# First layer begun with the values' projections, late modulation in buffers of its own, gated groups in four PSUM banks

## The chip, the cores and the metric

One core of one Trainium2 chip. The metric is the device time of one execution in microseconds (us). The engines are TensorE (PE), VectorE (DVE), ScalarE (ACT), GpSimd (POOL) and SyncE (SP), which issues every DMA of this kernel. Each runs its own instruction stream in order; semaphores tie them together. Everything is float32.

## The reference

A first block of two layers ("ab" and "cd") over 512 tokens x and 256 context tokens ctx, width 1024, and then a second block of two layers of feed-forward, mixing, feed-forward. The change touches only the first block; cut to that:

```python
def _adaln(cond, w_mod, b_mod):
    return jnp.split(jax.nn.silu(cond) @ w_mod + b_mod, 3, axis=-1)      # shift, scale, gate
def _post_norm(x, y, gate, g, b):
    return _layer_norm(ALPHA * x + gate * y, g, b)
def _ab_mixer(h, w_in, pool_w, pool_scale, sgu_w, sgu_b, w_out):
    a, ga, u, v, gb = split(h @ w_in)                                     # five times 512 columns
    ya = _multiscale_pool(a, pool_w, pool_scale) * jax.nn.silu(ga)        # windows 2, 4, 8, 16
    yb = _chunk_sgu(u, v, sgu_w, sgu_b) * jax.nn.silu(gb)                 # v normalized by head
    return jnp.concatenate([ya, yb], axis=-1) @ w_out
def first_block(x, c, ctx, c_ctx, ...):
    # layer ab
    sh, sc, gt = _adaln(c, ab_w_mod, ab_b_mod);  csh, csc, cgt = _adaln(c_ctx, ab_w_mod, ab_b_mod)
    y  = _ab_mixer(x * (1 + sc) + sh, ...);      yc = _ab_mixer(ctx * (1 + csc) + csh, ...)
    ctx = _post_norm(ctx, yc, cgt, ab_ln_g, ab_ln_b);  x = _post_norm(x, y, gt, ab_ln_g, ab_ln_b)
    # layer cd: Fourier mixing and latent attention, x attends to ctx and x
    h = x * (1 + sc2) + sh2;  hc = ctx * (1 + csc2) + csh2
    y = _cd_out(f_in, f_gate, attn, d_gate, cd_fnet_w, cd_w_out)
    return _post_norm(x, y, gt2, cd_ln_g, cd_ln_b)
```

## The kernel before

**Products.** Every dense product is taken in two parts: an operand is split into hi (ACT copies it to float32r) and lo (DVE subtracts hi from the operand), and PE does three matmuls, hi x hi, hi x lo, lo x hi (`mm3`). A weight chunk is 1024 x 256 (1 MB): SP loads it into one of two `raw` buffers, ACT makes `w_hi`, DVE makes `w_lo` (`split_at`, lines 1367 and 1785), into one of two pairs. `raws_to(n)` on SP loads up to chunk n, and waits before each load until the chunk two before it is split. ACT waits for the last use of the pair. Activations are held by feature, as `h_hi`, `h_lo` (x) and `ctx_hi`, `ctx_lo`.

**Order.** There is no scheduler in the first block: each engine's program is written out by hand, and a `Signal` counts events. PE takes PSUM banks from a ring of eight (`rot`); `claim` waits until the last holder of a bank was freed. ACT and DVE share three `work` tiles, given out by the list `work_order`.

**Layer ab.** (1) Eight modulation products of 1 MB of weights each (`mod_product`; weights into six `mod_w` buffers, then the last two), each turned to features (`mod_turn`); they give shift and scale. (2) Four x tiles of 128 tokens are turned by PE and scaled and split by ACT and DVE (`turn`). (3) Ten chunks of `ab_w_in` in order 0 to 9: chunks 0, 1 are the pool's input (kept in `pooled_in`), 2, 3 its gate, 4, 5 u, 6, 7 the values v, 8, 9 the second gate. A chunk other than 6 and 7 is four groups: two halves of 128 features, each for x (512 columns, 24 matmuls) and ctx (256 columns, 24 matmuls). Chunks 6, 7 are six token tiles each, with the weights as the moving operand; DVE then takes statistics and norm for each of 24 (chunk, tile, head) in turn, with POOL's power for the deviation. The ctx tiles are turned within chunk 0. (4) Sixteen late modulation products (`late_product`, numbers 8 to 23, the gate of ab and all of cd) lie between the groups; their weights go to `late_w`, which borrows the room of `u_gated` and `v_norm`, and for four of them to `raw`. (5) Meanwhile POOL makes the window means of `pooled_in`. (6) The middle: eight `pool` groups (g, r), where r = 0 is x and r = 1 ctx, and eight `sgu` groups; for each DVE multiplies by the gate, ACT makes hi, DVE makes lo, and only then comes the next. (7) Four chunks of `ab_w_out`, out-chunks 0 to 3: x tile i fills banks 2i and 2i+1; chunks 0 and 1 for all four tiles, then 2 and 3 tile by tile. The finished tile is called y(i). Then the same for ctx, with the layer norms (`AB_TAIL`) on DVE and ACT and turns of the normalized tiles back to features.

**Layer cd.** Eight chunks of `cd_w_in`. The ctx tiles are turned (`c_turn`) inside chunk 0; chunk 1 has two gate rows (PE multiplies a matrix of ones by diagonals that DVE builds at line 1837, `gate_diags`). POOL applies the gain and bias rows of ab's norm to X (lines 2404 and 2406). At the end of cd each tile's norm runs DVE statistics, POOL power, ACT normalize (line 1420), DVE gain (1874), POOL bias (2427), ACT square (1427), POOL power, DVE scale (1881), PE turn (815), while PE works on the next tile.

## Time and profile before

| | |
|---|---|
| median of 3 runs | 2972.14 us (2970.36 to 2980.99) |
| the profiled execution | 2969.76 us |
| its span, first to last instruction | 2968.0 us |
| PE, DVE, ACT, POOL busy | 94%, 39%, 32%, 6% |
| mean granted TensorE clock | 0.961 |

A matmul's end is modelled and matmuls are pipelined, so busy PE is not PE at its peak. The clock is given as a share of 2.4 GHz; the other level is 1.2 GHz. PEld is the weight load beside the matmul; SPq is the time of SP's DMA issue. "idle before <- X" names what ended an engine's idle time. L745 is the line of every matmul, so groups are told apart by tiles.

### The profile page before, as it was taken

The page shows a single profiled execution, that of the slowest core. Times are in us where ns is not written, and L with a number is a line of the kernel's source. Part 1 is how long each engine was busy: PE and PEld are TensorE (multiplying, and loading weights), DVE is VectorE, ACT ScalarE, POOL GpSimd, SP SyncE. Part 2 cuts the span into 40 slices and gives each one's busy share as a digit, 9 for nine tenths or more (in the row PEclk, how much of TensorE's full clock was granted, in tenths as well). Part 3 has the DMA queues.
Part 4 walks back from the last instruction along what each step waited for, and adds up shares of the span by engine and source line. Part 5 has one row for each costly group of instructions (what it writes and reads, how often), then busy time and mean ns, then how long its engine had stood idle before and what let it go on. Part 6 is the DMA issues. An engine that isn't in the chain of part 4 may idle for free.

```text
span 2968.0 us, 34969 instructions
## 1 busy us (share of the span) xinstructions
PE 2775.1 (94%) x14803; PEld 2220.0 (75%) x14803; DVE 1167.1 (39%) x1745; ACT 962.9 (32%) x1433; POOL 180.0 (6%) x291
## 2 busy tenths in 40 slices
PE   4998779998799999998799999999999998899998
PEld 2877668565688888776488888888888775688887
DVE  2123563255433324444643332433324445633322
ACT  2211232343232223545432222322225355332221
POOL 0130030000100000000000000000001000100000
PEclk7998989999899999998799999999999998899999
DMA  7432222002033323211123323223232111123321
GB/s 248 143 110 71 86 88 74 29 1 65 29 114 99 100 95 96 70 44 57 43 72 100 99 97 117 86 89 97 99 114 76 57 43 43 54 96 100 100 100 71
DMA packets 208000, 250.06 MB, mean 84 GB/s; under 512 B 6351, under 2 KB 187174, under 8 KB 207846
## 3 DMA queue, kind: packets, MB, share of 16 engines
q1 hardware_dynamic: 207846, 247.83, 25.9%
q8 instruction: 118, 1.93, 0.3%
q14 instruction: 36, 0.29, 0.0%
...
## 4 chain that ended last, share of the span: by engine, by line
PE 84%; DVE 6%; ACT 4%; issue 3%; POOL 1%; SPq 1%; DMA 1%; DVEq 0%; POOLq 0%; ACTq 0%
PE psum L745 81%; PE psum L1207 1%; PE psum L815 1%; PE psum L1128 1%; POOL stats_first L2362 1%; DVE w_lo L1785 1%; ACT w_hi L1367 1%; DMA mod_w<-in_ab_w_mod 0%; DVE h_lo L1794 0%; SPq L637 0%; DVE spare_lo L1785 0%; DVE v_norm L1958 0%; POOL X L2427 0%; ACT softplus L1737 0%; DVE stats_first L1861 0%
## 5 line engine op out<-in xcount | busy, mean ns | idle before, releaser
L745 PE MATMUL psum<-h_hi,w_hi 128*128 128x512 f32 (+1 forms) x2096 | 791.1, 377 | 28.1 <-issue 15.0
L745 PE MATMUL psum<-h_lo,w_hi 128*128 128x512 f32 (+1 forms) x2096 | 781.8, 373 | 0.0
L745 PE MATMUL psum<-h_hi,w_lo 128*128 128x512 f32 (+1 forms) x2096 | 781.3, 373 | 0.0
L1785 DVE TENSOR_TENSOR w_lo<-raw,w_hi 128x2048 fp32r<-128x2048 f32 (+1 forms) x176 | 400.0, 2275 | 767.2 <-ACT w_hi L1367 766.9
L745 PEld LDWEIGHTS psum<-h_hi,w_hi 128*128 128x128 f32 x2096 | 400.3, 191 | 106.4 <-issue 28.6
L745 PEld LDWEIGHTS psum<-h_hi,w_lo 128*128 128x128 f32 x2096 | 399.7, 191 | 68.5
L745 PEld LDWEIGHTS psum<-h_lo,w_hi 128*128 128x128 f32 x2096 | 400.3, 191 | 67.2 <-issue 1.2
L1367 ACT ACTIVATE w_hi<-raw 128x2048 fp32r<-128x2048 f32 (+1 forms) x176 | 332.6, 1892 | 219.1 <-PE psum L745 214.3
L1376 ACT ACTIVATE work<-psum 128x512 f32<-128x512 f32 (+3 forms) x184 | 91.5, 503 | 412.0 <-PE psum L745 348.0
L745 PE MATMUL psum<-w_hi,ff_hi 128*128 128x512 f32 x576 | 224.6, 390 | 0.0
L745 PE MATMUL psum<-w_lo,ff_hi 128*128 128x512 f32 x576 | 224.1, 389 | 0.0
L745 PE MATMUL psum<-w_hi,ff_lo 128*128 128x512 f32 x576 | 224.1, 389 | 0.0
L745 PE MATMUL psum<-w_hi,h_hi 128*128 128x256 f32 (+2 forms) x512 | 168.6, 329 | 27.5 <-DVE w_lo L1785 13.1
L1655 ACT ACTIVATE ff_hi<-work 128x512 fp32r<-128x512 f32 (+1 forms) x96 | 57.3, 597 | 367.8 <-DVE work L2183 367.8
L745 PE MATMUL psum<-w_lo,h_hi 128*128 128x256 f32 (+2 forms) x512 | 162.6, 318 | 0.0
L745 PE MATMUL psum<-w_hi,h_lo 128*128 128x256 f32 (+2 forms) x512 | 162.1, 317 | 0.0
L745 PEld LDWEIGHTS psum<-w_hi,h_hi 128*128 128x128 f32 x512 | 101.3, 198 | 41.8 <-issue 15.2
L2183 DVE TENSOR_TENSOR work<-work,psum 128x512 f32<-128x512 f32 (+1 forms) x96 | 61.7, 643 | 165.3 <-PE psum L745 165.2
L745 PEld LDWEIGHTS psum<-w_hi,ff_lo 128*128 128x128 f32 x576 | 108.1, 188 | 22.6
L745 PEld LDWEIGHTS psum<-w_hi,ff_hi 128*128 128x128 f32 x576 | 108.1, 188 | 22.4
L745 PEld LDWEIGHTS psum<-w_lo,ff_hi 128*128 128x128 f32 x576 | 108.1, 188 | 22.0
L745 PEld LDWEIGHTS psum<-w_hi,h_lo 128*128 128x128 f32 x512 | 100.9, 197 | 5.9
...
## 6 DMA issues: line engine op xcount, KB each, us to landing
raw<-in_ffn_w_gate SPq DMA_DIRECT2D x44, 1024.0 KB, 5.3
raw<-in_ffn_w_up SPq DMA_DIRECT2D x44, 1024.0 KB, 5.3
raw<-in_ffn_w_down SPq DMA_DIRECT2D x44, 1024.0 KB, 4.8
...
raw<-in_ab_w_in SPq DMA_DIRECT2D x10, 1024.0 KB, 5.2
mod_w<-in_ab_w_mod SPq DMA_DIRECT2D x8, 1024.0 KB, 11.7
raw<-in_w_out SPq DMA_DIRECT2D x8, 1024.0 KB, 4.9
raw<-in_cd_w_in SPq DMA_DIRECT2D x7, 1024.0 KB, 5.4
```

What stands on the lines that cost most here:

```text
L745: return pe.matmul(o, lhsT, rhs, start=start, stop=stop, skip_group_check=True)
L815: m = pe.transpose(bank(b, P, j * P), wide[1][:, k * P:(k + 1) * P], ident[:, :])
L1128: m = pe.transpose(bank(b + k // 4, P, (k % 4) * P), probs[(n - 1) % 2][:, k * P:(k + 1) * P], ident[:, :])
L1207: m = pe.transpose(bank(b, P, k * P), src[:, k * P:(k + 1) * P], ident[:, :])
L1367: act.activation(split_tiles(key)[0][:, 0:nk * n], raw[c % 2][:, 0:nk * n], ACT.Copy).then_inc(*w_hi_made.mark(key))
L1376: act.activation(o, src, func, **kw).then_inc(*kept.mark(name or event))
L1655: act.activation(ff_hi[:, k, off:off + n], work[used.index((k, half_)) % 3][:, 0:n], ACT.Copy).then_inc(*ff_hi_made.mark(event))
L1785: dve.tensor_tensor(lo[:, 0:nk * n], raw[c % 2][:, 0:nk * n], hi[:, 0:nk * n].bitcast(F32), ALU.subtract).then_inc(*w_lo_made.mark(key))
L2183: dve.tensor_tensor(w, w, full(event, n), ALU.mult).then_inc(*gated.mark(event))
L2362: pool.tensor_tensor(o, a, half[:, 0:n], ALU.pow).then_inc(*rsqrt_made.mark(event))
```

## The change

- **Order of chunks.** 6, 7, 0, 1, 2, 3, 4, 5, 8, 9. The order on PE, ACT and DVE comes from one list, `AB_STEPS`. Values are projected tile by tile for both chunks as soon as an x tile is turned; turns of the tiles and late modulations 8 to 13 lie between. Numbers 14 to 21 lie in chunks 0 and 1, 22 and 23 in chunk 2.
- **DMA.** The wait of SP for the vectors' turn goes. All eight modulation weights have buffers and are issued first; X comes in four tiles with a weight chunk between; late modulation weights have three buffers (`u_gated`, `silu_ga`, one of its own) and leave `raw`.
- **Values' norm.** Four heads of a tile at once: four statistics, four aggregates, one bias, one power on POOL, four norms.
- **Weight splits.** Each is placed one chunk ahead (`split`), also those of chunks 8 and 9.
- **Middle.** Groups in banks 4 to 7, r = 0 before r = 1; product n+1 comes before lo n on DVE. PE does the output tiles 0 and 1 of out-chunks 0 and 1 between them. Out-chunk 2's spare tiles are free after the pool groups.
- **cd.** Context turns after chunks 0 and 1, not inside; gate diagonals behind a weight split; the gain and bias rows of X on DVE in chunks 1 and 2. At the end of cd the norm is two DVE instructions, (x - mean) g and then times the deviation plus b; ACT's and POOL's parts go.

```diff
+AB_STEPS = [("turn", 0), ("turn", 1), ("v", 6, 0), ("v", 7, 0), ("turn", 2), ("mod", 8), ("v", 6, 1), ("v", 7, 1), ("turn", 3), ("mod", 9),
+            ("v", 6, 2), ("v", 7, 2), ("turn", 4), ("mod", 10), ("v", 6, 3), ("v", 7, 3), ("turn", 5), ("mod", 11), ("sgu_w",),
+            ("v", 6, 4), ("v", 6, 5), ("end", 6), ("split", 0), ("mod", 12), ("v", 7, 4), ("v", 7, 5), ("end", 7), ("mod", 13)]
+for _i, _ch in enumerate((0, 1, 2, 3, 4, 5, 8, 9)):
+    if _ch < 9:
+        AB_STEPS.append(("split", (1, 2, 3, 4, 5, 8, 9)[_i]))
+    for _j in range(2):
+        for _r in range(2):
+            AB_STEPS.append(("group", _ch, _j, _r))
+            if _ch < 2:
+                AB_STEPS.append(("mod", 14 + 4 * _ch + 2 * _j + _r))
+            if _ch == 2 and _r == 0:
+                AB_STEPS.append(("mod", 22 + _j))
+            if _ch in (4, 5) and _r == 0:
+                AB_STEPS.append(("gate", _ch - 4, _j))
+    AB_STEPS.append(("end", _ch))
+AB_MID = [(kind, g, r) for kind in ("pool", "sgu") for r in range(2) for g in range(4)]
...
-            sp.wait_ge(*psum_full["vecs"])
-            for n in range(6):
+            for n in range(8):
                 sp.dma_start(mod_w[n][:, :, :], mod_chunk("ab_w_mod", n * CW)).then_inc(*mod_landed[n].mark(n))
+            for t in range(NT):
+                sp.dma_start(X[:, t, :], A["x"][0, t * P:(t + 1) * P, :]).then_inc(*x_landed[t].mark("all"))
+                if t == 1:
+                    raws_to(0)
+            raws_to(1)
             sp.dma_start(CTX[:, :, :], A["ctx"][0].rearrange("(t p) d -> p t d", p=P)).then_inc(*ctx_landed.mark("all"))
...
             def late(m):
-                s = m % 2 if m < 8 else 1
-                if m > 1:
-                    sp.wait_ge(*psum_full["modp", 8 + (m - 2 if m < 8 else m - 1)])
+                s = m % 3 if m < 14 else 0
+                before = {14: 12, 15: 14}.get(m, m - 3)
+                sp.wait_ge(*psum_full["modp", 8 + before if m > 2 else 7])
...
+            for m in range(3):
+                late(m)
+            sp.dma_start(sgu_w[:, :, :], A["ab_sgu_w"][0].rearrange("h i j -> i h j")).then_inc(*sgu_w_landed.mark("all"))
...
+            raws_to(3)
+            for m in range(3, 8):
+                late(m)
+            raws_to(4)
+            late(8)
+            late(9)
+            raws_to(5)
+            for m in range(10, 14):
+                late(m)
+            raws_to(6)
+            inv_count(0)
+            raws_to(7)
+            late(14)
+            late(15)
+            inv_count(1)
+            raws_to(8)
+            inv_count(2)
+            inv_count(3)
+            raws_to(9)
             raws_to(CHUNK["ab_out", 0] + 2)
             sp.wait_ge(*h_lo_made["sgu", 3, 1])
...
-            raws_to(CHUNK["cd_in", 0] + 3)
-            sp.wait_ge(*h_lo_made["ct", NC - 1, 1])
+            raws_to(CHUNK["cd_in", 0] + 5)
+            sp.wait_ge(*ln_made["ab_x", NT - 1])
...
+            for r in range(2):
+                for g in range(4):
+                    pool_group(g, r)
             for c in range(2):
                 begin(("ab_out", c))
-                for i in range(NT):
+                for i in range(2):
+                    m = out_part("ab_x", c, i, i * P)
+                if c == 0:
+                    pe.wait_ge(*sgu_w_turned["all"])
+                    pe.wait_ge(*v_normed[5])
+                for hd in range(4):
+                    sgu_group(hd, c)
+            for c in range(2):
+                for i in range(2, NT):
                     m = out_part("ab_x", c, i, i * P)
                 done(m, ("chunk", "ab_x", c))
...
-                act.wait_ge(*h_lo_made["sgu", 3, 1])
+                act.wait_ge(*h_lo_made["pool", 3, 1])
...
+            def v_norms(t):
+                heads = [4 * t + hd for hd in range(4)]
+                places = [full(("v", 6 + hd // 2, t), P, hd % 2 * P) for hd in range(4)]
...
+                for i, ps in zip(heads, places):
+                    m = dve.bn_stats(stat("v", i, 0, 6), ps)
...
+                bias_variance(("v", t), v_stat(t, 7), 1.0)
+                dve.wait_ge(*rsqrt_made["v", t])
+                for hd, i, ps in zip(range(4), heads, places):
+                    m = dve.tensor_scalar(v_norm[:, t, hd * P:(hd + 1) * P], ps, stat("v", i, 6, 7), stat("v", i, 8, 9), ALU.subtract, ALU.mult)
...
+            for n, event in enumerate(AB_MID):
+                if event == ("sgu", 0, 0):
+                    split_at(CHUNK["ab_out", 1])
...
+                mid_product(event)
+                if n:
+                    mid_lo(AB_MID[n - 1])
...
             for ch in range(8):
+                if ch:
+                    split_at(CHUNK["cd_in", ch] + 1)
                 if ch == 1:
                     for j in range(2):
                         gate_diags(("gate_cd", j), mod_cd, j, 0)
-                if ch:
-                    split_at(CHUNK["cd_in", ch] + 1)
+                if ch in (1, 2):
+                    x_rows(2 * ch - 2)
+                    x_rows(2 * ch - 1)
+                if ch < NC:
+                    turn("ct", ch, h_hi, h_lo, L + ch * P, scale_odd[:, :, 1], shift_odd[:, :, 1])
...
+                if s == "cd":
...
+                    dve.scalar_tensor_tensor(out=tile, in0=tile, scalar=stat("ln", i, 12, 13), in1=g_row[:, :], op0=ALU.subtract,
+                                             op1=ALU.mult).then_inc(*residual.mark(("gain", s, t)))
+                    dve.wait_ge(*residual["gain", s, t])
+                    dve.wait_ge(*rsqrt_made["ln", s, t])
+                    dve.scalar_tensor_tensor(out=tile, in0=tile, scalar=stat("ln", i, 14, 15), in1=cd_b[:, :], op0=ALU.mult,
+                                             op1=ALU.add).then_inc(*ln_put.mark(t))
+                    return
```

## Rows read from the trace of the kernel before

**Rows 1.** Busy time by stage: PE, PEld, DVE, ACT, POOL, then clock, DMA share, GB/s.
```profile
0.00:67.90 67.90, 24.01 (x194) 14.01 (x194) 16.44 (x39) 18.84 (x37) 3.19 (x7) 0.80 0.75 245
67.90:294.80 226.90, 212.13 (x1384) 177.40 (x1384) 58.62 (x156) 43.40 (x70) 48.73 (x50) 0.95 0.35 114
294.80:355.00 60.20, 43.49 (x206) 33.55 (x206) 31.65 (x50) 16.46 (x22) 0.00 (x0) 0.89 0.31 105
401.30:445.70 44.40, 31.13 (x118) 23.71 (x118) 30.24 (x37) 13.97 (x22) 21.55 (x10) 0.81 0.40 127
```

**Rows 2.** Timeline of the start (start us, us, engine, line, op; idle before).
```profile
6.17 11.31 SPq L637 DMA_DIRECT2D mod_w<-in_ab_w_mod  x6
11.56 2.77 PE L745 MATMUL psum<-mod_w,silu_c 128*32 128x256 f32 x16 [5.42 <-DMA mod_w<-in_ab_w_mod]
44.99 2.77 PE L745 MATMUL psum<-mod_w,silu_c 128*32 128x256 f32 x16 [16.40 <-DMA mod_w<-in_ab_w_mod]
67.90 0.77 PE L745 MATMUL psum<-h_hi,w_hi 128*128 128x512 f32 x1 [13.31 <-issue]
```

**Rows 3.** Timeline of PE, end of chunk 5.
```profile
187.53 0.80 PE L745 MATMUL psum<-h_hi,w_hi 128*128 128x512 f32 x1
193.47 1.49 PE L745 MATMUL psum<-v_norm,silu_c 128*32 128x256 f32 x16
194.89 0.38 PE L745 MATMUL psum<-ctx_hi,w_hi 128*128 128x256 f32 x1
197.86 0.50 PE L745 MATMUL psum<-mod_sum,mod_row 96*128 96x2 f32 x4
```

**Rows 4.** Timeline of DVE, first head of the values.
```profile
201.38 0.30 DVE L1951 BATCH_NORM_STATS2 stats_first<-psum 128x6 f32<-128x128 f32 x1 [2.04 <-PE psum L745]
202.76 0.41 DVE L1958 TENSOR_SCALAR v_norm<-psum,stats_first 128x128 f32<-128x128 f32 x1 [0.67 <-POOL stats_first L2362]
```

**Rows 5.** Waits of PE, 190 to 300 (us in total, times, longest).
```profile
PE psum L745 <- DVE w_lo L1785: 14.8, 3, 6.0
```

**Rows 6.** Timeline of DVE, the gated groups.
```profile
299.50 0.74 DVE L1991 SCALAR_TENSOR_TENSOR work<-psum,cols,silu_ga 128x512 f32<-128x512 f32 x1
318.68 0.69 DVE L1794 TENSOR_TENSOR h_lo<-work,h_hi 128x512 fp32r<-128x512 f32 x1 [0.69 <-ACT h_hi L1411]
333.90 0.42 DVE L1794 TENSOR_TENSOR ctx_lo<-work,ctx_hi 128x256 fp32r<-128x256 f32 x1 [0.48 <-ACT ctx_hi L1411]
```

**Rows 7.** Timeline of the middle: PE's first output tile, the fourth out-chunk's hi.
```profile
324.23 0.77 PE L745 MATMUL psum<-w_hi,h_hi 128*128 128x512 f32 x1 [11.37 <-issue]
343.92 1.92 ACT L1367 ACTIVATE spare_hi<-raw 128x2048 fp32r<-128x2048 f32 x1 [7.57 <-DMA raw<-in_ab_w_out]
```

**Rows 8.** Timeline of DVE: gate diagonals of either layer, a context split.
```profile
155.23 0.88 DVE L1837 TENSOR_SCALAR work<-ident,mod 128x128 f32<-128x128 f32 x4
421.20 4.27 DVE L1794 TENSOR_TENSOR ctx_lo<-work,ctx_hi 128x512 fp32r<-128x512 f32 x2 [2.64 <-ACT ctx_hi L1403]
430.92 5.81 DVE L1837 TENSOR_SCALAR work<-ident,mod_odd 128x128 f32<-128x128 f32 x8
```

**Rows 9.** Waits of PE, 345 to 470.
```profile
PE psum L745 <- DVE work L1837: 10.0, 1, 10.0
PE psum L799 <- DVE work L1854: 3.1, 1, 3.1
```

**Rows 10.** Timeline of the first tile's norm at the end of cd.
```profile
744.71 1.23 DVE L1874 TENSOR_TENSOR X<-X,g_row 128x1024 f32<-128x1024 f32 x1 [1.31 <-ACT X L1420]
746.08 2.42 POOL L2427 TENSOR_TENSOR X<-X,b_row 128x1024 f32<-128x1024 f32 x1 [2.87 <-DVE X L1874]
752.14 1.94 PE L815 MATMUL psum<-ident,wide 128*128 128x128 f32 x8 [3.29 <-DVE wide L1881]
```

**Rows 11.** The page's costliest groups: the low half of a weight split.
```profile
L1785 DVE TENSOR_TENSOR w_lo<-raw,w_hi 128x2048 fp32r<-128x2048 f32 (+1 forms) x176 | 400.0, 2275 | 767.2 <-ACT w_hi L1367 766.9
```

**Rows 12.** DMA issues, 0 to 500 (KB each, median us to landing).
```profile
raw<-in_ab_w_in SPq DMA_DIRECT2D x10, 1024.0 KB, 5.2
```

More of the change, by code:

```diff
@@ L115, in add @@
         plan.append(what)
-    for ch in range(10):
+    for ch in (6, 7, 0, 1, 2, 3, 4, 5, 8, 9):
         add(("ab_in", ch), "ab_w_in", 0, "cols", ch * CW, CW, True)
-        if ch > 5:
-            w, c0 = LATE_MOD[6 + ch]
-            add(("mod", 14 + ch), w, 0, "cols", c0, CW, False)
     for c in range(4):
@@ L870, in tensor_program @@
             mod_turn(7)
-            pe.wait_ge(*x_landed["all"])
-            for t in range(NT):
-                turn("xt", t, X[:, t, :])
             open_turn = []
@@ L925, in tensor_program @@
-                end(("ab_in", ch))
-            pe.wait_ge(*raw_landed[CHUNK["mod", 23] % 2][CHUNK["mod", 23]])
-            late_product(23, raw[CHUNK["mod", 23] % 2][:, :].rearrange("p (k n) -> p k n", n=CW))
-            close_turn()
-            pe.wait_ge(*pool_w_landed["all"])
-            pe.wait_ge(*pooled[3])
-            for g in range(4):
-                for r, (off, n) in enumerate(RANGES):
-                    b = claim(rot.take(), ("pool", g, r))
-                    done(mm(bank(b, n), pool_w[:, g, :], pooled_in[:, g, PAD_OFF[r]:PAD_OFF[r] + n], True, True), ("pool", g, r))
@@ L937, in tensor_program @@
-            pe.wait_ge(*sgu_w_turned["all"])
-            pe.wait_ge(*v_normed[7, 5, 1])
-            for hd in range(4):
-                for r, (off, n) in enumerate(RANGES):
-                    b = claim(rot.take(), ("sgu", hd, r))
-                    for q in range(n // P):
-                        m = mm(bank(b, P, q * P), v_norm[:, off // P + q, hd * P:(hd + 1) * P], sgu_wT[:, hd, :], True, True)
-                    done(m, ("sgu", hd, r))
-            def ab_ready(i, k, h):
-                if i == 0 and h == 0:
-                    pe.wait_ge(*h_lo_made[("pool", k, 1) if k < 4 else ("sgu", k - 4, 1)])
+                elif kind == "group":
+                    _, ch, j, r = step
+                    w = begin(("ab_in", ch)) if j == r == 0 else weights(("ab_in", ch))
+                    project(("ab", ch, j, r), w, j * P, P, h_hi, h_lo, *RANGES[r], rot)
+                    if (ch, j, r) == (2, 1, 1):
+                        close_turn()
+                elif kind == "gate":
+                    gate_row(("gate", step[1], step[2]))
+                elif kind == "end":
+                    end(("ab_in", step[1]))
@@ new lines, in tensor_program, with pool_group, sgu_group @@
+            mid = Ring([4, 5, 6, 7])
+            def pool_group(g, r):
+                off, n = RANGES[r]
+                b = claim(mid.take(), ("pool", g, r))
+                done(mm(bank(b, n), pool_w[:, g, :], pooled_in[:, g, PAD_OFF[r]:PAD_OFF[r] + n], True, True), ("pool", g, r))
+            def sgu_group(hd, r):
+                off, n = RANGES[r]
+                b = claim(mid.take(), ("sgu", hd, r))
+                for q in range(n // P):
+                    m = mm(bank(b, P, q * P), v_norm[:, off // P + q, hd * P:(hd + 1) * P], sgu_wT[:, hd, :], True, True)
+                done(m, ("sgu", hd, r))
@@ L950, in out_part, with ab_ready @@
+            def ab_ready(k):
+                pe.wait_ge(*h_lo_made[("pool", k, 0) if k < 4 else ("sgu", k - 4, 0)])
             def out_part(s, c, i, off):
@@ L2368, in gpsimd_program @@
             pool.memset(pooled_in[:, :, :], 0.0).then_inc(*zeroed.mark("all"))
+            for t in range(6):
+                rsqrt(("v", t), v_stat(t, 8), v_stat(t, 7), 4)
             for g, window in enumerate(POOL_WINDOWS):
```

401 lines of the change are left out of this document (172 added, 229 removed).

## The prediction

> **What bounds the kernel now.** I read the page first: TensorE (PE) is busy 94% of 2968.0 us, so only its idle and slow-clock time can be won. The diff touches the first layer and the end of the second ("cd"), so next came busy time by stage [rows 1]. PE is idle 43.9 us before its first projection at 67.9, 14.8 us inside the ten input chunks, 16.7 us between the last chunk and the first finished output tile y0 (294.8 to 355.0), and 13.3 us in the first two cd chunks. Then the timeline and the waits, to see who ends each gap.
>
> *Start* [rows 2]. The modulation products wait for data: number 6 waits 16.40 us because X, CTX and two weight chunks (5 MB) sit ahead of it. From the first landing (11.56) to that one (44.99) 11 MB come in: 3.04 us per MB, a full queue. After the last product PE stands 13.3 us while ACT and DVE scale and split four x tiles and then two weight chunks.
> *Chunks* [rows 3 to 5]. Chunks 6 and 7 (the values) make PE outrun DVE's norm chain; it waits 14.8 us in three pieces for weight splits queued on DVE behind that chain.
> *Middle* [rows 6, 7]. The gated groups are a product, ACT's hi and DVE's lo in strict turn, 34.8 us on DVE (299.50 to 334.3). PE's output tiles wait for their banks (11.37 us).
> *Start of cd* [rows 8, 9]. PE waits 10.0 us for the gate diagonals. Eight of them take DVE 5.81 us here, four took 0.88 us at 155.23; POOL is busy 21.55 us in this stage with X's gain and bias rows.
> *End of cd* [rows 10]. Each tile's chain ACT norm, DVE gain, POOL bias, ACT square, POOL rsqrt, DVE scale is longer than PE's 11 us of matmuls.
>
> **The change, part by part** (microseconds from the span's start; new kernel's times are worked out).
>
> *1. Start.* SP no longer waits for the vector rows, so modulation weights are issued some 1.9 us earlier (6.17 back to about 4.3) and all eight MB come first. First landing 9.65, the eighth 9.65 + 7 x 3.0 = 30.7. Then 2.8 us of product and turn and 1.5 us of one-plus-scale: 35. At 3.04 us per MB [rows 2] X tile 0, tile 1, weight chunk 6 land at 32.2, 33.7, 36.7, then tiles 2 and 3 and chunk 7 at 42.7, CTX at 45.8, late modulations behind. Tile 0 is scaled and split by 38.5 (an estimate: a scaling of 1.5, hi 0.6, two lo's of 0.69 [rows 6]). Chunk 6's hi (1.9) and lo (2.2) [rows 11] follow: values of tile 0 start at about **42**. Chunk 7's hi waits for its landing, its lo is done at 46.9, about when PE, cold, ends the first group. Dense work thus starts 25.9 us earlier than 67.9.
>
> *2. Values phase.* Per token tile PE has two value groups of 256 columns (24 matmuls, 2.97 each [rows 3]), one turn of x (0.95), one late modulation (1.42 + 0.37): 8.5 us. DVE has per tile four heads of statistics and norm. In turn they cost 1.7 each [rows 4], 6.8 together; batched, 4 x 0.3 + 4 x 0.2 + 0.2 + 0.7 for POOL + 4 x 0.35 make about 4.3. The x turn adds 3.2: 7.5 in all, under 8.5, with some 3 us between a tile's split and its use. So I cost the normalization at nothing. Its cover gone (1.7 a head) it costs 6 x 1.5 = 9 us. Six tiles, sgu turn and the last modulation: PE reaches chunk 0 at **94**. The banks hold: eight claims pass before a value bank is reused, by then its norm is done.
>
> *3. Chunks 0 to 5, 8, 9.* A chunk is 2 x (5.65 + 2.97) = 17.2 us [rows 3]; modulations 14 to 21 add 8 x 1.8, so chunks 0 and 1 end at 142.8. The 14.8 us of waits and about 6 us of slow clock behind them (0.95 over 226.9 us) go, since each weight split now starts a chunk ahead on a DVE with nothing behind. A new wait appears: SP queues modulation 22 behind weight chunk 5, whose buffer is free only when chunk 3 is split. That split waits for chunk 1's end (142.8), then hi 1.9 and lo 2.2: SP issues at t0+4.9. One MB lands 5.2 after issue [rows 12], the one behind it 3.04 later: t0+13.2. PE wants it at t0+5.6, so 7.6 us of stall, and the clock falls: 1.5 more. I take **9.1**; bounds 0 (if PE came later) and 12. Queued behind SP's wait there are only the next window's inverse counts, needed 100 us later. Modulation 23 is issued after product 22 and lands 3 us before PE asks. (By the Trainium skill, DMA: Bandwidth & Descriptors, the section on the anatomy of a DMA by the GpSimd path, a transfer costs about 2.0 us plus bytes at 436 GB/s; two MB would then be in at 6.8 us, the stall 6.1 instead of 7.6 and the sum 1.5 better. It is a fit for another issuing path and I go by the rows.)
> Chunk 2 then ends at 172.7, 3 at 189.9, 4 and 5 (two gate rows each, 0.8 a piece) at 227.5, 9 at **261.9**. Before it was 294.8: **-32.9**. Check by differences: -25.9 start, -14.8 waits, -6 clock, +1.8 for modulation 23 inside, +1.9 for two x turns inside, +9.1: -33.9.
>
> *4. Middle.* T is the last chunk's end. The first product on DVE still comes at T+4.8, behind a weight split (299.50 against 294.8). Pipelined, with product n+1 covering ACT's hi of n, a 512-wide pool group costs 0.74 + 0.69 instead of 2.1, a 256-wide one about 0.95. DVE: pool r=0 done T+10.2, r=1 T+14, split of out-chunk 1 T+18.2, sgu r=0 T+26.4, r=1 T+32 (27 us against 34.8). PE: tiles 0 and 1 with out-chunk 0 from T+9.8, sgu groups, out-chunk 1, tiles 2 and 3, so 22 us of output matmuls are done by T+38.8 rather than waiting for the whole chain. Out-chunk 3 is late next: SP loads it only after the last sgu lo (T+32) and behind two row loads; before, its hi started 9.6 us after that lo (334.3 to 343.92 [rows 7]). Hi 1.9 and lo 2.2 make T+46, y0 ends T+**48.8** after 4 us of stall. Before: 60.2. **-11.4**; bounds -15 (load at 5.2) and -5.
> From y0 to cd chunk 0, before 355.0 to 401.3, the order and the pieces of work are the same on every engine: 0.
>
> *5. First cd chunks.* Gain and bias rows go from POOL to DVE (8 x 1.3 = 10.3 us), in chunks 1 and 2 behind the diagonals, beside 11 us of PE per chunk whose next weights have 4 us of slack: nothing. Context turns come after whole chunks. From cd start U: DVE's last context norm U+13.8, ct turn, ACT's hi of chunk 2's weights U+20.6, lo U+23, diagonals U+23.9 (0.9 as at 155.23). PE is at the gate row at U+17.6, waits 6.3 instead of 10.0, and a wait of 3.1 in the context turns goes [rows 9]. Chunk 1 with its turn ends U+33.9 against U+44.3: **-10.4**. This rests on DVE's slow rows being POOL's doing; if they are not, 0. (The Trainium skill, SBUF — State Buffer, section "SBUF: two separate sides", says that GpSimd and a DVE instruction with two SBUF inputs exclude each other for a whole instruction. By that rule the two ctx splits, 4.27 us at 421.20 when 1.3 is usual, shrink as I assume; it also lets no such block in elsewhere, as DVE's splits beside the window sums have a chunk of slack.)
>
> *6. End of cd.* Between statistics and scaled tile, ACT's 1.24 with its two hops and POOL's 2.42 go, DVE's gain runs beside POOL's rsqrt, a second 1.29 on DVE is added: the statistics are there at 742.6 (2.1 before the gain row: 1.3 for ACT, 0.8 for POOL's rsqrt and the bias), the scaled tile at 748.8 instead of 752.0, 3.2 per tile. Four tiles make 12.8, less what PE's 11 us per tile takes back: PE's wait of 3.29 at tile 0 is all gone, the later ones shrink. **-12**, bounds -9 and -13.
>
> Sum: 32.9 + 11.4 + 10.4 + 12 = 66.7. The profiled execution took 2969.76 (1.76 around its span, 2.4 below the median 2972.14): 2969.8 - 66.7 = **2903**.
>
> **Rivals.**
> *A. Values phase bound by DVE or landings.* The chain is not shortened by batching, or data come late and the phase starts at 47. Against: the queue's pace in rows 2. 9 + 5 + some clock: 2915 to 2932.
> *B. No stall at modulation 22*, and out-chunk 3 early: 9 + 4: 2890.
> *C. Start of cd unchanged* and the middle still waits as before (the change does not do what it says there): +10.4 + 11.4: 2925; with A, up to 2940.
> *D. Slower than before.* One mechanism: late modulations starve PE. Thirteen of them (11 to 23) now hang on three buffers reloaded only after a product, in one SP queue. Slack is about 14 us after an issue. To lose 66.7 + 15 they must land 14 + 82/13 = 20 us after issue; singly they took 5.2, 11.7 only in the opening burst. At 22 us: 13 x 8 = 104, so 3007.
>
> **How the numbers follow.** Forecast (2890 to 2914) 0.57; A 0.17; C 0.09; B or better 0.10; no more than 0.5% from before 0.04; D 0.03. Half a per cent (15 us) is about what a measurement of this kernel can tell. Faster 0.93, same 0.04, slower 0.03. Leaving out the top 0.1 and the bottom 0.07, the range is 2882 to 2931.
>
> **What would show it.** First value matmul near 42; no PE wait over 1 us between 50 and 142; one wait near 148 of 5 to 9 us ended by a late modulation's DMA; last chunk's end near 262; y0 near 311 after a wait for out-chunk 3's lo; cd's gate diagonals 0.9 us for four; cd tiles 3 us apart less. Wrong if the first value matmul is after 50, or if PE waits on v_norm or h_lo in every tile.

## The result

The changed kernel takes 2907.28 us (median of 4 runs, 2906.6 to 2908.55) against 2971.25 for the kernel before on the same chip (4 runs, 2970.0 to 2980.99): ratio 0.9784, 95% interval 0.9773 to 0.9796. That is 64 us or 2.2% faster. The forecast was 2903.0 with a range of 2882 to 2931.

### The profile after, by stage

Busy time by stage of the changed kernel (columns as in [rows 1]). The stages have moved: the values' phase is 45 to 98, chunks 0 and 1 98 to 148, the other six chunks 148 to 268 (two rows), the middle 268 to 315, and most of the start of cd (359.6 to 393.8) lies in 358 to 392.

```profile
0.00:45.00 45.00, 24.41 (x178) 14.64 (x178) 7.95 (x20) 10.88 (x19) 3.18 (x7) 0.87 0.95 319
45.00:98.00 53.00, 52.36 (x436) 46.69 (x436) 32.60 (x103) 17.20 (x37) 5.07 (x5) 0.95 0.68 222
98.00:148.00 50.00, 50.00 (x357) 38.13 (x353) 8.48 (x24) 10.67 (x18) 1.85 (x2) 1.00 0.54 177
148.00:175.00 27.00, 20.23 (x97) 16.25 (x96) 2.88 (x3) 3.66 (x5) 11.38 (x10) 0.75 0.38 131
175.00:268.31 93.31, 93.21 (x539) 79.75 (x537) 18.09 (x29) 20.51 (x30) 20.16 (x17) 1.00 0.16 54
268.31:315.02 46.71, 40.98 (x186) 31.71 (x187) 30.47 (x49) 16.11 (x21) 0.00 (x0) 0.96 0.30 102
358.00:392.00 34.00, 27.81 (x114) 21.85 (x113) 21.68 (x38) 10.69 (x14) 1.10 (x2) 0.90 0.23 72
```

Against [rows 1] PE's idle time ahead of the first projection is 20.6 us and not 43.9, the queue is busy 95% of the start and not 75%, and the projections run without a gap except in one stage: between 148 and 175 PE stands 6.8 us and its clock is at 0.75. PE's own list of waits, up to 345, says who ends them (us in total, times, longest; the waits for the modulation weights and the identity matrix at the start, 10.2 and 5.7 us, are left out, and all others are 2.5 us or less):

```profile
PE psum L781 <- DMA u_gated<-in_cd_w_mod: 6.8, 1, 6.8
PE psum L781 <- DVE w_lo L1809: 4.6, 1, 4.6
PE psum L781 <- DVE spare_lo L1809: 3.1, 1, 3.1
```

The 14.8 us of waits for weight splits inside the chunks [rows 5] are gone; the one w_lo wait left is the first values' matmul. Here it is on the timeline, with what ACT and DVE did before it (start us, us, engine, line, op; idle before):

```profile
40.62 1.89 ACT L1403 ACTIVATE w_hi<-raw 128x2048 fp32r<-128x2048 f32 x1
42.55 2.29 DVE L1809 TENSOR_TENSOR w_lo<-raw,w_hi 128x2048 fp32r<-128x2048 f32 x1 [1.11 <-ACT w_hi L1403]
44.90 0.58 PE L781 MATMUL psum<-w_hi,h_hi 128*128 128x256 f32 x1 [4.64 <-DVE w_lo L1809]
```

It answers to the 67.90 of [rows 2]: 23.0 us sooner. The values' norms, one token tile with its four heads and the next tile's turn, on DVE (it answers to [rows 4]):

```profile
61.80 0.89 DVE L1963 BATCH_NORM_STATS2 stats_first<-psum 128x6 f32<-128x128 f32 x4 [1.56 <-PE psum L781]
...
64.45 1.36 DVE L1973 TENSOR_SCALAR v_norm<-psum,stats_first 128x128 f32<-128x128 f32 x4 [1.13 <-POOL stats_first L2413]
65.73 1.36 DVE L1849 TENSOR_SCALAR work<-psum,one_plus_scale,mod 128x128 f32<-128x128 f32 x4
...
70.49 0.89 DVE L1963 BATCH_NORM_STATS2 stats_first<-psum 128x6 f32<-128x128 f32 x4 [1.94 <-PE psum L781]
```

Four heads take 4.0 us from 61.80 to 65.8, a tile 8.7 us from one set of statistics to the next, and the idle time ahead of each set of statistics ends on PE: DVE waits for PE, not the other way round.

The new wait of chunk 2, on SP's and PE's timelines:

```profile
153.19 0.37 SPq L649 DMA_DIRECT2D raw<-in_ab_w_in  x1
153.60 0.58 SPq L675 DMA_DIRECT2D u_gated<-in_cd_w_mod  x1
160.88 2.35 PE L781 MATMUL psum<-u_gated,silu_c 128*32 128x256 f32 x14 [6.78 <-DMA u_gated<-in_cd_w_mod]
```

The two issues stand 0.4 us apart with weight chunk 5 in front, as the prediction read the queue. The middle's end, which answers to [rows 7]:

```profile
309.56 2.29 DVE L1809 TENSOR_TENSOR spare_lo<-raw,spare_hi 128x2048 fp32r<-128x2048 f32 x1 [6.53 <-ACT spare_hi L1403]
311.90 0.50 PE L781 MATMUL psum<-spare_hi,h_hi 128*128 128x512 f32 x1 [3.09 <-DVE spare_lo L1809]
```

The start of cd, which answers to [rows 8] and [rows 9]:

```profile
377.71 1.29 DVE L1818 TENSOR_TENSOR ctx_lo<-work,ctx_hi 128x512 fp32r<-128x512 f32 x2 [3.11 <-ACT ctx_hi L1439]
379.96 2.29 DVE L1809 TENSOR_TENSOR w_lo<-raw,w_hi 128x2048 fp32r<-128x2048 f32 x1 [0.96 <-ACT w_hi L1403]
382.17 1.65 DVE L1861 TENSOR_SCALAR work<-ident,mod_odd 128x128 f32<-128x128 f32 x8
383.18 2.04 PE L781 MATMUL psum<-work,ones 128*128 128x512 f32 x2 [6.19 <-DVE work L1861]
```

Eight diagonals take 1.65 us (5.81 before), two context splits 1.29 (4.27 before), and the gate wait is 6.2 (10.0 before). The end of cd, which answers to [rows 10]:

```profile
690.68 1.28 DVE L1895 SCALAR_TENSOR_TENSOR X<-X,stats_first,g_row 128x1024 f32<-128x1024 f32 x1
692.49 1.28 DVE L1899 SCALAR_TENSOR_TENSOR X<-X,stats_first,b_row 128x1024 f32<-128x1024 f32 x1 [0.52 <-POOL stats_first L2413]
697.40 1.06 PE L851 MATMUL psum<-ident,wide 128*128 128x128 f32 x8 [0.39 <-DVE wide L1911]
```

PE's wait there was 3.29 and is 0.39; over the four tiles its waits for the scaled tile are 16.2 us before and 7.3 after.

### Where the time came from

To compare stages I follow six marks on DVE's timeline through both kernels: the last gated product of chunk 9; the statistics of the first output tile's norm (y0); of the second context norm; of cd's first and last norm; and the last residual addition of the first feed-forward. Each time is the start of that instruction.

| mark | before | after | gained in this stage |
|---|---|---|---|
| last gated product of chunk 9 | 295.4 | 268.8 | 26.6 |
| y0's norm | 358.0 | 317.8 | 13.6 |
| second context norm | 412.6 | 370.8 | 1.6 |
| cd's first norm | 740.9 | 689.0 | 10.1 |
| cd's last norm | 793.8 | 732.6 | 9.3 |
| first feed-forward's last addition | 1165.6 | 1101.0 | 3.4 |
| mixing of layer 0, addition to addition | 358.5 long | 353.8 long | 4.7 |
| mixing of layer 1 | 351.1 long | 358.1 long | -7.0 |

64.6 us are won by 1101; 62.4 arrive in the span (2968.0 against 2905.6). The difference is in the two mixing stages, whose code did not change; more on that below. The 1.6 us between y0 and the context norm are no gain of the change either: with the same code there, the kernels below take 52.9 to 53.0 us in seven profiles and 54.6 to 54.9 in five, and the kernel before took 54.6.

### The profile page after: what moved, and what is told of

It is laid out like the page before. It is cut to its first block, busy times and chain, and to the rows that moved or that the text cites. A ratio compares the mean times of both kernels' runs of the same rounds, so it can differ in the third digit from the quotient of the medians.

```text
span 2905.6 us, 34955 instructions
## 1 busy us (share of the span) xinstructions
PE 2769.2 (95%) x14803; PEld 2216.7 (76%) x14803; DVE 1162.3 (40%) x1735; ACT 957.5 (33%) x1429; POOL 143.4 (5%) x261
## 4 chain that ended last, share of the span: by engine, by line
PE 87%; DVE 5%; ACT 3%; issue 2%; DMA 1%; SPq 1%; POOL 1%; DVEq 0%; POOLq 0%; ACTq 0%
PE psum L781 84%; PE psum L1243 1%; PE psum L1164 1%; PE psum L851 1%; ACT w_hi L1403 1%; SPq L662 0%; DVE w_lo L1809 0%; DMA mod_w<-in_ab_w_mod 0%; DVE spare_lo L1809 0%; DVE h_lo L1818 0%; POOL stats_first L2413 0%; DVE stats_first L1885 0%; DVE work L1878 0%; ACT softplus L1761 0%; ACT softplus L1763 0%
## 5 line engine op out<-in xcount | busy, mean ns | idle before, releaser
L781 PE MATMUL psum<-w_hi,h_hi 128*128 128x256 f32 (+2 forms) x512 | 168.2, 329 | 13.7 <-DVE w_lo L1809 11.7
L1679 ACT ACTIVATE ff_hi<-work 128x512 fp32r<-128x512 f32 (+1 forms) x96 | 57.3, 596 | 367.3 <-DVE work L2234 367.3
L781 PEld LDWEIGHTS psum<-w_hi,ff_lo 128*128 128x128 f32 x576 | 108.1, 188 | 22.2
```

The costliest lines, as they stand in the source:

```text
L781: return pe.matmul(o, lhsT, rhs, start=start, stop=stop, skip_group_check=True)
L1679: act.activation(ff_hi[:, k, off:off + n], work[used.index((k, half_)) % 3][:, 0:n], ACT.Copy).then_inc(*ff_hi_made.mark(event))
```

## The experiments

All are the changed kernel with one edit (e9 with three), timed in five rounds against the kernel before. Runs of one kernel scatter in steps of 3 to 10 us (for instance 2901.6, 2901.6, 2908.1 and 2910.8 for the same one), so for the smaller effects the marks of the profiled execution decide; here they are for every run, with the length of layer 0's mixing stage.

| kernel | median us | chunk 9 | y0 | context | cd first | cd last | ffn | mixing 0 |
|---|---|---|---|---|---|---|---|---|
| changed | 2907.28 | 268.8 | 317.8 | 370.8 | 689.0 | 732.6 | 1101.0 | 353.8 |
| e1 | 2894.74 | 257.2 | 306.6 | 359.5 | 677.9 | 721.5 | 1089.9 | 353.9 |
| e2 | 2904.84 | 268.8 | 314.4 | 367.3 | 685.8 | 729.4 | 1099.1 | 359.1 |
| e3 | 2906.98 | 267.2 | 317.5 | 372.2 | 684.1 | 727.7 | 1097.3 | 358.6 |
| e4 | 2922.3 | 278.3 | 326.5 | 379.4 | 697.0 | 740.6 | 1109.3 | 361.2 |
| e5 | 2923.84 | 267.0 | 317.3 | 372.1 | 689.5 | 743.5 | 1115.2 | 358.1 |
| e6 | 2914.3 | 268.8 | 324.3 | 377.2 | 695.6 | 739.2 | 1109.0 | 359.1 |
| e7 | 2925.7 | 268.9 | 319.1 | 373.9 | 702.7 | 746.4 | 1116.0 | 358.8 |
| e8 | 2908.92 | 266.9 | 314.6 | 367.6 | 686.1 | 729.7 | 1098.1 | 353.8 |
| e9 | 2885.07 | 257.6 | 302.0 | 356.6 | 668.5 | 712.1 | 1079.2 | 358.1 |
| e10 | 2917.5 | 266.5 | 325.3 | 378.2 | 695.5 | 739.2 | 1107.9 | 357.9 |
| e11 | 2912.4 | 270.0 | 320.1 | 375.0 | 693.3 | 736.9 | 1105.3 | 353.8 |

Kernels with the same code up to chunk 9 reach it at 266.5 to 268.9, and those with the same code in the middle go from there to y0 in 47.7 to 50.3 us (changed, e1, e3, e4, e5, e7, e8, e11): differences under some 3 us in a stage prove nothing by themselves.

### e1: modulation 22 ahead of weight chunk 5

```diff
-            raws_to(7)
-            late(14)
+            late(14)
+            raws_to(7)
```

> The changed kernel, but modulation 22's weights are issued ahead of weight chunk 5, not behind the wait for its buffer. My theory: the 6.78 us wait ahead of product 22 at 160.9 goes and the slow clock behind it (0.79 from 143 to 175) with it: 2907.3 falls by 7 to 8.5, to about 2899.5, and PE has no wait over 1 us between 100 and 175. Rival, the landing is slow for another reason (queue full of other loads, weight chunk 5 now late): another wait of 3 us or more by chunk 5, sum within 2 us of 2907.

2894.74 us (2893.86 to 2896.41), ratio 0.9746 (0.9733 to 0.9759): 12.5 us under the changed kernel, more than I gave it. The weights are now issued at 142.5 instead of 153.6. By the timelines, the weight split after chunk 2's starts 11.7 sooner (171.2 against 182.9), 0.7 of which stood before chunk 2. So the disputed wait costs **11.0 us**: 6.8 of standing, 4.2 of slow clock behind it. Windows through that place, changed kernel first (columns as in [rows 1]):

```profile
153.00:158.00 5.00, 1.11 (x5) 0.57 (x4) 0.16 (x1) 0.60 (x1) 1.30 (x2) 0.85 0.75 249
158.00:163.00 5.00, 2.12 (x14) 0.94 (x16) 0.00 (x0) 0.00 (x0) 0.00 (x0) 0.50 0.48 170
163.00:170.00 7.00, 7.00 (x33) 6.42 (x30) 0.16 (x1) 0.41 (x2) 0.47 (x1) 0.50 0.59 206
170.00:171.00 1.00, 1.00 (x5) 0.77 (x5) 0.00 (x0) 0.35 (x1) 1.00 (x1) 0.91 0.00 0
171.00:178.00 7.00, 7.00 (x46) 5.16 (x45) 0.16 (x1) 0.98 (x2) 4.96 (x6) 1.00 0.01 2
```

and e1:

```profile
153.00:158.00 5.00, 5.00 (x45) 3.86 (x45) 0.16 (x1) 0.98 (x2) 0.64 (x1) 1.00 0.91 301
158.00:163.00 5.00, 5.00 (x25) 4.16 (x24) 0.00 (x0) 0.38 (x1) 1.88 (x2) 1.00 0.53 197
```

PE's clock, the last but two of the columns, falls to 0.50 (1.2 GHz) during the wait and is back at 1.00 only from 171, though PE works without a gap from its return at 160.88. At half clock up to 170 and 0.91 in the next microsecond, 2.1 x 0.5 + 7 x 0.5 + 1 x 0.09 = 4.6 us of that work is lost, close to the 4.2 that e1 gives back. Neither weight chunk 5 nor anything else became late in turn: the rival is out.

### e2: output chunk 3 ahead of the rows

```diff
-            raws_to(CHUNK["ab_out", 0] + 2)
+            raws_to(CHUNK["ab_out", 0] + 3)
             sp.wait_ge(*h_lo_made["sgu", 3, 1])
```

> The changed kernel, but output chunk 3's weights are issued ahead of SP's wait for the last gated group and of the gain and bias rows. My theory: its lo part is made before 306 instead of at 309.6, PE's wait of 3.1 us at 311.9 goes: about -3, 2904. Rival: DVE is the limit there (it has the last lo parts to make until 300.7), then the wait shrinks by at most 1 us and the time stays 2907.

2904.84 us (2901.55 to 2910.8), ratio 0.9781 (0.9768 to 0.9795), which alone tells nothing. In the trace y0's norm comes at 314.4, 3.4 sooner from the same 268.8, and all marks up to cd's end keep 3.2 to 3.5 of it. DVE now makes both lo parts back to back:

```profile
300.71 4.49 DVE L1809 TENSOR_TENSOR spare_lo<-raw,spare_hi 128x2048 fp32r<-128x2048 f32 x2 [1.39 <-ACT spare_hi L1403]
```

PE's wait of 3.09 for the second of them is gone, and up to 300.7 this profile runs as the changed kernel's does. The wait is the late load's, as forecast, and costs 3.4; measured against the shortest of the other kernels in this stage (47.7 us, here 45.6) some 2 us are left of it.

### e3: gate diagonals ahead of the split

```diff
+                if ch == 1:
+                    for j in range(2):
+                        gate_diags(("gate_cd", j), mod_cd, j, 0)
                 if ch:
                     split_at(CHUNK["cd_in", ch] + 1)
-                if ch == 1:
-                    for j in range(2):
-                        gate_diags(("gate_cd", j), mod_cd, j, 0)
```

> The changed kernel, but cd's gate diagonals are made ahead of the split of cd weight chunk 2 (as in the kernel before), the rows of x behind both. My theory: what is left of the gate wait is DVE's order; the diagonals come 2.3 to 3 us earlier, the 6.2 us wait becomes 3 to 4, sum -2.5 (2904.8). Rival: the wait belongs to POOL or ACT (the turn's hi part), then the diagonals can't come earlier: within 1 us of 2907.

2906.98 us (2900.27 to 2910.18), ratio 0.9779 (0.9766 to 0.9793). From the context norm to cd's first norm it takes 311.9 us instead of 318.3: 6.3 less, against 2.5 expected. The gate's matmul:

```profile
381.36 1.10 PE L781 MATMUL psum<-work,ones 128*128 128x512 f32 x2 [2.94 <-DVE work L1861]
```

The wait fell by 3.25, as DVE's order said; the other 3 us are the clock: the two matmuls take 1.10 us and not 2.04, and the granted clock from 358 to 392 is 1.00 where it was 0.90. A wait of 2.9 us left the clock alone here, one of 6.2 did not. The total hardly shows it: of the 6.3 us, 3.7 stand at the feed-forward's end, the rest going in stages of the same code at another clock, and layer 0's mixing takes 4.8 more.

### e4: norms head by head

```diff
-                for i, ps in zip(heads, places):
-                    m = dve.bn_stats(stat("v", i, 0, 6), ps)
...
+                for hd, i, ps in zip(range(4), heads, places):
+                    dve.bn_stats(stat("v", i, 0, 6), ps).then_inc(*v_stats.mark((t, hd, 0)))
+                    dve.wait_ge(*v_stats[t, hd, 0])
+                    dve.bn_aggr(stat("v", i, 6, 8), stat("v", i, 0, 6)).then_inc(*v_stats.mark((t, hd, 1)))
+                    dve.wait_ge(*v_stats[t, hd, 1])
+                    bias_variance(("v", t, hd), stat("v", i, 7, 8), 1.0)
+                    dve.wait_ge(*rsqrt_made["v", t, hd])
...
```

> The changed kernel, but the values' heads are normalized one after the other (1.7 us each in the kernel before) and not four at a time (4.0 us for four now). My theory: DVE's work for a tile grows from about 7 to 9.7 us against PE's 8.7, so the values' phase becomes DVE's: +1 us per tile, +5 to +9 in all, 2912 to 2916. Rival, DVE's slack and the eight banks cover it: within 1.5 us of 2907.

2922.3 us (2916.23 to 2923.4), ratio 0.9834 (0.982 to 0.9847): 15.0 above the changed kernel. Chunk 9 ends at 278.3 instead of 268.8, +9.5 (the prediction's price for this was 9). At the feed-forward's end 8.3 of it stand, and layer 0's mixing at 361.2 against 353.8 adds 7.4 that this edit doesn't touch. The clean measure is the phase itself, from the first values' matmul to the first of chunk 0: 62.9 us (43.91 to 106.84), where all the other kernels with the new order take 52.6 to 53.8. On DVE a tile's statistics now start every 9.4 us (61.79, 71.24) instead of 8.7. PE does not pay for it tile by tile, as the forecast had it: DVE falls behind, and PE waits twice late in the phase, for ctx_lo (at 90.2) and for v_norm (at 106.8):

```profile
PE psum L781 <- DVE ctx_lo L1818: 5.6, 1, 5.6
PE psum L781 <- DVE v_norm L1969: 2.2, 1, 2.2
```

### e5: cd's norm as before

```diff
-            down("cd", KT, lambda i: None)
+            down("cd", KT, lambda i: normalize("cd", i, X[:, i, :]))
...
+                pool.wait_ge(*residual["gain", "cd", t])
+                pool.tensor_tensor(X[:, t, :], X[:, t, :], cd_b[:, :], ALU.add).then_inc(*ln_made.mark(("cd", t)))
```

> The changed kernel with the LayerNorm at cd's end as in the kernel before (normalize on ACT, gain on DVE, bias on POOL, and ACT's part queued behind the last tile's turned halves). My theory: the four tiles' waits become 3.3, 2.3, 4.3 and 6.3 again and the time rises by 12, to 2919 (clock included). Rival, the gain at cd's end came from the earlier parts (for instance x's rows being ready sooner): within 3 us of 2907.

2923.84 us (2921.37 to 2926.73), ratio 0.9832 (0.9813 to 0.9851): 16.6 above. By the marks the cd end takes 53.9 us instead of 43.6 between the first and the last norm and the feed-forward 3.4 us more, **13.7** together; 4.3 are again the mixing stage. Other kernels take 367.1 to 369.8 us from cd's last norm to the feed-forward's end, this one 371.7 and the kernel before 371.8, so those 3.4 us are the norm's too. PE's waits for the scaled tile, 686 to 760 in the changed kernel and 686 to 775 in this one:

```profile
PE psum L851 <- DVE wide L1911: 7.3, 4, 3.9
```

```profile
PE psum L851 <- DVE wide L1905: 17.2, 4, 6.4
```

The four waits are 3.4, 3.7, 3.7 and 6.4 us, not quite those of the kernel before; their sum is 17.2 where it was 16.2.

### e6: outputs after the groups

```diff
             for c in range(2):
-                begin(("ab_out", c))
-                for i in range(2):
-                    m = out_part("ab_x", c, i, i * P)
                 ...
             for c in range(2):
-                for i in range(2, NT):
+                begin(("ab_out", c))
+                for i in range(NT):
                     m = out_part("ab_x", c, i, i * P)
```

> The changed kernel, but TensorE computes all gated groups first and the first two output tiles' parts behind them; DVE's order, made one group ahead, stays. My theory: outputs beside the groups hide DVE's work of 16 groups, so TensorE waits again for the gated groups' banks and lo parts: +6 to +9, 2913 to 2916. Rival: DVE made one group ahead is what bought the 13.5 us of the middle, the outputs' place does nothing: within 2 us of 2907.

2914.3 us (2908.17 to 2920.57), ratio 0.9797 (0.9776 to 0.9818). From chunk 9's end to y0's norm 55.5 us instead of 49.0: **+6.5** (+5.2 to +7.8 against the 47.7 to 50.3 of the same middle), and the feed-forward's end is 8.0 later. PE's windows from 266 to 316, changed kernel first:

```profile
266.00:316.00 50.00, 44.27 (x210) 34.64 (x209) 32.10 (x52) 16.25 (x22) 0.00 (x0) 0.97 0.31 102
```

```profile
266.00:316.00 50.00, 43.06 (x181) 33.38 (x181) 30.99 (x50) 16.18 (x22) 0.00 (x0) 0.86 0.30 105
```

Little more idle time (1.2 us), but 0.11 less clock over 50 us: the waits, short and many in both, let the clock fall when no output work lies between them.

### e10: the lo part right behind its own product

```diff
                 mid_product(event)
-                if n:
-                    mid_lo(AB_MID[n - 1])
-            mid_lo(AB_MID[-1])
+                mid_lo(event)
```

> The changed kernel, but DVE makes each gated group's lo part right behind its own product, waiting for ACT's hi part, and not one group later. Outputs stay beside the groups. My theory: the middle gained 13.5 us, 6.4 of them by the outputs' place; the one-group lead carries the rest, so y0's norm, at 317.8 in the changed kernel, comes 6 to 8 us later, 2914. Rival, the outputs hide DVE's turn-round too: within 1.5 us of 2907.

2917.5 us (2916.04 to 2924.1), ratio 0.9822 (0.9805 to 0.9839). Chunk 9 to y0: 58.8 us instead of 47.7 to 50.3: **+8.5 to +11.0**. So both halves of the middle's change carry it, and the lead of one group probably more than the outputs' place. Together they come to 14 to 19 where 13.6 were gained; either each is worth more with the other in place, or it is scatter. Both undone at once were not run, nor were the four banks and the order of the groups undone alone.

### e7: rows of x on POOL

```diff
-                if ch in (1, 2):
-                    x_rows(2 * ch - 2)
-                    x_rows(2 * ch - 1)
...
+            for t in range(NT):
+                pool.wait_ge(*psum_full["xo", t, 1])
+                pool.tensor_tensor(X[:, t, :], X[:, t, :], ab_g[:, :], ALU.mult).then_inc(*ln_made.mark(("gain", t)))
...
```

> The changed kernel, but the rows' gain and bias of x are back on POOL (8 operations of 2.4 us) beside cd chunks 0 and 1. My theory: DVE's gate diagonals take 4 to 5 us instead of 1.65 for the eight and its lo parts 4.3 instead of 1.3 while POOL runs, the gate wait is 9 to 10 us instead of 6.2: +4 to +8, 2911 to 2915. Rival: the slow DVE rows had another cause (ACT, banks) and the gain of 10.1 us there came from the order: within 2 us of 2907.

2925.7 us (2921.16 to 2927.45), ratio 0.9835 (0.9816 to 0.9854): 18.4 above; by the marks the stage takes 328.9 us instead of 318.3, **+10.6**, the rest is mixing (5.0) and early scatter. The gate wait is 18.15 us, twice what I expected. DVE and POOL in that stage:

```profile
376.25 2.36 DVE L1903 SCALAR_TENSOR_TENSOR stats_first<-stats_first 128x1 f32<-128x1 f32 x1 [0.66 <-POOL stats_first L2400]
378.54 1.36 DVE L1849 TENSOR_SCALAR work<-psum,one_plus_scale_odd,shift_odd 128x128 f32<-128x128 f32 x4
383.02 3.67 DVE L1818 TENSOR_TENSOR ctx_lo<-work,ctx_hi 128x512 fp32r<-128x512 f32 x2 [3.13 <-ACT ctx_hi L1439]
386.62 4.42 DVE L1809 TENSOR_TENSOR w_lo<-raw,w_hi 128x2048 fp32r<-128x2048 f32 x1
390.96 7.91 DVE L1861 TENSOR_SCALAR work<-ident,mod_odd 128x128 f32<-128x128 f32 x8
```

```profile
376.18 2.41 POOL L2437 TENSOR_TENSOR X<-X,g_row 128x1024 f32<-128x1024 f32 x1
388.97 4.27 POOL L2439 TENSOR_TENSOR X<-X,b_row 128x1024 f32<-128x1024 f32 x1
398.24 2.05 PE L781 MATMUL psum<-work,ones 128*128 128x512 f32 x2 [18.15 <-DVE work L1861]
```

An instruction on a single column, 0.16 us long elsewhere, takes 2.36, which is the length of POOL's row beside it (376.18 to 378.59); a weight split takes 4.42 instead of 2.29, the eight diagonals 7.91 instead of 1.65, while the turn that reads PSUM keeps its 1.36 us. POOL is held up in turn: one of its rows takes 4.27 instead of 2.4, and ends 2.2 us behind the weight split (393.24 against 391.04), as if it had begun only then. The Trainium skill, SBUF — State Buffer, section "SBUF: two separate sides", calls the shared pair "an **exclusive lock**, not a bandwidth split", held for the whole instruction; the trace agrees in these rows.

### e8: the first chunk's split ahead of the turn

```diff
+            split_at(CHUNK["ab_in", 6])
             act.wait_ge(*scale_made["ab"])
...
                     if t == 0:
-                        split_at(CHUNK["ab_in", 6])
                         split_at(CHUNK["ab_in", 7])
```

> The changed kernel, but the first values' weight chunk is split ahead of the first tile's turn, on ACT and DVE both. My theory: the first values' matmul, at 44.9 now behind a lo part of 42.6 to 44.8, comes at about 42.5 to 43, but the second chunk lands at 43.3 and its lo part stays at 47.5, so TensorE waits there: -1 us, 2906. Rival A, the split was on the path of all that follows: -2.4. Rival B, the chunk isn't there by 36: the turn is held up and the time rises by 1 to 3.

2908.92 us (2904.46 to 2910.0), ratio 0.9778 (0.9759 to 0.9797): no gain. The chunk's hi part now shows when the data are there:

```profile
37.62 1.91 ACT L1403 ACTIVATE w_hi<-raw 128x2048 fp32r<-128x2048 f32 x1 [3.58 <-DMA raw<-in_ab_w_in]
44.62 0.55 PE L781 MATMUL psum<-w_hi,h_hi 128*128 128x256 f32 x1 [8.05 <-issue]
```

The chunk lands at 37.6 (36.7 in the prediction), the turn behind its split is late in exchange, and the first matmul is at 44.6. Chunk 9 ends at 266.9, within the spread of 266.5 to 268.9. The turn is held up, as rival B had it, but by no more than the split now saves: the two are work in a row on the same two engines, whichever goes first.

### e11: SP waits for the vectors

```diff
+            sp.wait_ge(*psum_full["vecs"])
             for n in range(8):
```

> The changed kernel, but SP again waits for the transposed vector rows before it issues the modulation weights. My theory: all loads shift by 1.9 us (issue 6.2 and not 4.2), the queue is what sets the start, so the first values' matmul and all behind it come 1.9 later: 2909.2. Rival, the start is set by ACT's and DVE's order (turn, then split) and not by landings: no change at the first values' matmul, 2907.

2912.4 us (2909.97 to 2917.84), ratio 0.9803 (0.9787 to 0.9819). The first weights are issued at 6.15 instead of 4.22, the first values' matmul is at 45.95 (44.90 in the changed kernel, 43.27 in e3), chunk 9 ends at 270.0 (266.5 to 268.9 without the wait): a shift of 1.1 to 3.5, which holds the 1.9 expected. The landing of the eighth modulation weight shows it best: 34.0, against 31.7 to 32.4 in the other eleven profiles of the new order. The start without the wait has its first values' matmul anywhere from 43.1 to 45.2, so this one profile speaks for the theory but does not settle it. The rest of the 5.1 between the medians falls later, in stages where the same code differs anyway.

### e9: three moves together

The edits of e1, e2 and e3 in one kernel.

> The changed kernel with three moves of order: modulation 22's weights ahead of weight chunk 5 (alone: 11 us sooner behind it), output chunk 3 ahead of the rows (3.4 sooner at the first norm), gate diagonals ahead of the split (6.3 sooner between the context's norm and cd's end). My theory: they lie in different stages and add up, 2907.3 - 11.0 - 3.4 - 6.3 = 2886.6. Rival: a move only shifts the wait to the next late thing (the split of cd chunk 2 behind the diagonals, weight chunk 5 behind modulation 22), then 2890 to 2895. The layers' mixing stages, whose length differs by 4 to 7 us from run to run, put 3 us of scatter on both.

**2885.07 us** (2881.12 to 2889.77), ratio 0.9705 (0.9691 to 0.972): 22.2 under the changed kernel and 86 under the kernel before. By the marks cd's last norm is at 712.1 instead of 732.6 (-20.5, of the 20.7 that the three add up to), the first feed-forward ends 21.8 sooner. The rival, a wait that only moves on, would have left 12 to 17. The longest waits of PE between 266 and 400:

```profile
PE psum L781 <- DVE work L1861: 2.9, 1, 2.9
PE psum L781 <- ACT work L1434: 2.5, 1, 2.5
```

### The mixing stages

Layer 0's mixing takes 353.8 us in four of these profiles and 357.9 to 361.2 in the other nine, the kernel before's included; layer 1's takes 351.1 in the kernel before. The work is the same. Windows of 50 us in the changed kernel, then in e2, which has 359.1:

```profile
1200.00:1250.00 50.00, 48.87 (x327) 37.02 (x326) 22.44 (x41) 29.49 (x50) 3.39 (x8) 1.00 0.16 43
```

```profile
1200.00:1250.00 50.00, 48.87 (x292) 36.32 (x291) 19.65 (x39) 28.62 (x47) 3.37 (x8) 0.90 0.15 43
```

PE is busy 48.87 us in both, at clock 1.00 in one and 0.90 in the other: 0.1 x 48.9 = 4.9 us of work less, which is nearly all of the 5.3 between the two stages (between 1300 and 1400 the clocks differ too, 0.90 and 0.69 against 0.84 and 0.72). Why the chip grants one or the other there was not tried; it is no effect of the change, since both lengths occur among kernels that differ nowhere near this stage.

## Why the prediction was right

The total came out 4.3 us above the forecast, by several errors of both signs: -6.3 at chunk 9's end and +2.2 in the middle are the largest. That they cancel in part is luck, and so are 1.6 us gained and 2.3 us lost in stages that the change doesn't touch.

- **1, start.** Forecast 42, measured 44.90, in other runs of the same start 43.1 to 45.2. The landings came 1 to 1.5 us later than reckoned (the eighth modulation weight at 32.1 and not 30.7, weight chunk 6 at 37.7 and not 36.7), and one-plus-scale was done at 37.85 and not at 35. In e3, where PE's clock between 34 and 39 was 1.00, it was done at 36.4; in the changed kernel's profile the clock was 0.50. So half of the error is the landing and half the clock. The term is 1.1 to 3.2 too large.
- **2, values phase.** Forecast 52 us for the phase, measured 53.8 (44.90 to 98.65). The pace was given as 8.5 us a tile, though its terms (5.94, 0.95, 1.42 and 0.37) add up to 8.7; measured are 8.2 to 8.7. The clock, 0.50 in the first 5 us and 0.83 in the next, cost some 2.9 us, which the sum had left out; the rest of the phase was about 1 us shorter than forecast. That DVE's norms are hidden only when batched was right, and e4 measured its price at 9.2 in the phase against 9, though as two waits and not 1.5 us in every tile.
- **3, chunks.** The wait at modulation 22 was where and whose I said, 6.78 us instead of 7.6, the transfer landing 7.7 after the issue ahead of it (forecast 8.3). The clock behind it was mis-sized: 1.5 forecast, 4.2 measured by e1. Together 11.0 instead of 9.1, inside the bounds of 0 to 12. With the start and the values' phase, chunk 9's end gained 26.6 instead of 32.9. This is the largest error, 6.3 us, made of 2.9 at the start, 1.8 in the values' phase and 1.9 here, and it is mostly of one kind: work at half clock beside or after a wait that I priced by the wait alone. (By the fit in the Trainium skill, DMA: Bandwidth & Descriptors, section "Anatomy of one DMA — SWDGE (gpsimd) path", which is for another issuing path, the two megabytes would by estimate have been in 6.8 us after the issue. The trace's 7.7 lies between that and my 8.3.)
- **4, middle.** 13.6 instead of 11.4; the late load of output chunk 3 cost 3.4 (e2) against 4. That the two parts carry it is shown by e6 and e10. The excess of 2.2 lies on the path that the prediction drew, from the chunk's end at 268.3: the last gated lo part is done 31.0 us behind it (299.35, forecast 32), out-chunk 3's hi part starts 8.3 us later (307.61) and not 9.6 as in the kernel before, and its lo part is done at 43.5 and not at 46. The clock, 0.96 here where it was 0.89 [rows 1], is another matter: PE waits for that lo part in any case.
- **y0 to the start of cd.** Forecast 0, measured 1.6, which is within what the same code takes from run to run (52.9 to 54.9 us).
- **5, start of cd.** 10.1 against 10.4, the gate wait 6.19 against 6.3. The doubt, whether DVE's slow rows are POOL's doing, is settled by e7. I had priced the wait that was left at its length; e3 took 3.25 us off it by order alone and gained 6.3, the rest being clock.
- **6, end of cd.** 9.3 between the norms and 3.4 behind them, 12.7 against 12. Undone alone (e5) it costs 13.7.
- Rival A's mechanism exists (e4) but was not this kernel's; B is what e1 and e2 made of it, though 2890 was their sum by my prices and e9 with the gate's order gives 2885; C and D did not happen, no late modulation but number 22 made PE wait.
- The other 2.3 us were given back in unchanged code, in the mixing stages, by the clock and not by the change.
